# Expert jobs of a hybrid decoder step: the order of the weight splits at a job's start and in the pass of chunk 1

## The chip, the cores and the metric

One core of a Trainium2 chip runs the whole program in one launch. The metric is the device time of one execution in microseconds (us), the median over several runs. The core has a matmul engine (TensorE, "PE" in the profile, its weight loads "PEld"), a vector engine (VectorE, "DVE"), a scalar engine (ScalarE, "ACT"), GpSimd ("POOL") and a sync engine (SyncE, "SP") that here only issues transfers. Each runs its own instructions in program order and waits for the others on semaphores.

## The reference

The kernel computes one step of a two-layer decoder for 256 prompt tokens and 32 sample tokens (288 columns), model width 1024. Layer 0 is a Mamba-2 and sliding-window attention mixer followed by a dense SwiGLU. Layer 1 is an RWKV-7 mixer followed by a mixture of experts, and only this last stage is touched:

```
logits = h @ router                      # 8 experts
top_v, top_i = top_k(logits, 2); gates = softmax(top_v)
for e in range(8):
    y += combine[e] * ((silu(h @ wg[e]) * (h @ wu[e])) @ wd[e])   # 1024 -> 2816 -> 1024, float32
```

## The kernel before

**Jobs and chunks.** The chosen tokens are gathered into jobs of at most 128 rows, each with one expert; with the given inputs there are eight jobs, numbered 0 to 7 here. Job 0 is the first, jobs 1 to 6 are the body of a hardware loop, job 7 is the last and has extra work for the final sum. The expert's hidden width of 2816 is cut into FC = 11 chunks of 256. A chunk's weights are 6144 columns of float32 on 128 partitions: 4096 for gate and up together ("gu", 2 MB) and 2048 for down ("dn", 1 MB). They come into four slots in turn (MS = 4; slot 0 is in the buffer `arena`, the others are in `ring`), by SP's `load_part` (L825 to L831), in the order gu c, dn c-1, gu c+1, and so on. SP waits before each issue until the slot's last user has finished: for gu it is ScalarE that signals this, in its pass of that chunk, after `gu_full`; for dn it is the end of `down`.

**Splits.** TensorE multiplies in a rounded 32-bit format, so every operand is split in two: a head (the rounded value, copied by ScalarE in `heads`, L1411, with its instructions at L1423 for gu and L1418 for dn) and a rest (value minus head, by VectorE in `rests`, L2138, with L2149 for gu and L2143 for dn). Each product is three matmuls: head by head, head by rest, rest by head. A gu chunk is split in two pieces of 2048 columns, numbered 0 and 1; only chunk 0 is split in four pieces of 1024.

**A chunk on TensorE.** `up(c)` is 24 matmuls of 512 columns into bank c mod 2, 12 for each piece. ScalarE takes silu of the gate half (L1486), VectorE multiplies it with the up half (L2291; this also signals `gu_free`). `turn(c)` transposes the product (L3127, two matmuls), ScalarE copies the head of the turned activation (L1493, "turned head" below) and VectorE subtracts for its rest (L2307, "turned rest", signals `tr_free`). `down(c)` is 12 matmuls that add into banks 3 and 4; it waits for the turned rest of its chunk and for the rest of its dn weights. TensorE's order in a job is up(0), up(1), turn(0), up(2), down(0), turn(1), up(3), down(1), turn(2), ... up(10), down(8), turn(9), turn(10), the transposes of the next job's tokens (`turn_tokens`, L3080), down(9), down(10). Then up(0) of the next job follows at once.

**The order on ScalarE and VectorE** is written out by hand in their `job` functions (L1466 and L2282). At the start of a job that is not the first, ScalarE makes the four heads of chunk 0, evicts the finished rows of the previous job (`rows_out`, L1435 and L1436, which waits for the previous job's down(10)), and makes the two heads of chunk 1. VectorE makes the rests of chunk 0 and of piece 0 of chunk 1, then waits for silu(0), multiplies, and makes the rest of piece 1 of chunk 1. After that both go through a loop with one pass for each chunk c: silu or product of chunk c, then head or rest of piece 0 of chunk c+2, the turned activation of chunk c-1, piece 1 of chunk c+2, and a dn part (ScalarE's of chunk c at the end, VectorE's of chunk c-1 near the start). So in the pass of chunk 1 the turned activation of chunk 0 stands behind piece 0 of chunk 3 on both engines, and on VectorE also behind the dn rest of chunk 0.

Of the kernel before, what the change touches and what calls it, by code (L numbers as in the profile page):

```python
# [5 lines left out]
F32 = mybir.dt.float32  # L6
# [3 lines left out]
ALU = mybir.AluOpType  # L10
ACT = mybir.ActivationFunctionType
# [21 lines left out]
FC = FF // 256  # L33
# [96 lines left out]
def decoder_trunk(nc, a, out):  # L130
    with ExitStack() as ctx:
# [5 lines left out]
        def sem(name):  # L137
            if name not in sems:
                sems[name] = ctx.enter_context(nc.semaphore(name))
            return sems[name]  # L140
# [248 lines left out]
        def turned(c):  # L389

            return ps[:, 2 if c % 2 == 0 else 7, 0:256]
# [37 lines left out]
        first = []  # L429
# [607 lines left out]
        def _(act):  # L1037
            A = nc.scalar.activation
# [372 lines left out]
            def heads(j, c, part, pieces):  # L1411

                s = c % MS
                act.wait_ge(sem(f"{part}_loaded{s}"), 16 * (uses[s] * j + c // MS + 1))
                if part == "dn":
                    if c >= 3:
                        act.wait_ge(sem(f"dn_slot_free{(c - 3) % MS}"), uses[(c - 3) % MS] * j + (c - 3) // MS + 2)
                    A(down_head(c), mslot[s][:, GU:SLOT], ACT.Copy).then_inc(sem("dn_head"), 1)  # L1418
                    return
                for i in pieces:  # L1420
                    w = piece_width(c, part)
                    o = i * w
                    A(mhead[c % 2][:, o:o + w], mslot[s][:, o:o + w], ACT.Copy).then_inc(sem("gu_head"), 1)  # L1423
# [7 lines left out]
            def rows_out(j):  # L1431

                act.wait_ge(sem(f"dn_slot_free{(FC - 1) % MS}"), uses[(FC - 1) % MS] * j + 1)
                act.wait_ge(sem("ysb_free"), j)
                A(ysb[:, 0:512], ps[:, 3, :], ACT.Copy)  # L1435
                A(ysb[:, 512:1024], ps[:, 4, :], ACT.Copy).then_inc(sem("y_out"), 1)  # L1436
# [20 lines left out]
            A(gt[:, 1, :], gt[:, 0, :], ACT.Exp).then_inc(sem("gate_exp"), 1)  # L1457
            load_functions(SILU)

            def pair_scale(c):  # L1460

                n = TOK[c][1]
                act.wait_ge(sem(f"pair_loaded{c}"), 32)
                A(pair[0][c][0:n, :], pair[0][c][0:n, :], ACT.Copy, scale=gt[0:n, 2, c:c + 1]).then_inc(sem("pair_scaled"), 1)

            def job(j, first, last=False):  # L1466
                if first:
                    heads(j, 1, "gu", range(2))
                    for u in range(2):
                        token_heads(j, u)  # L1470
                else:
                    heads(j, 0, "gu", range(4))
                    rows_out(j)
                    heads(j, 1, "gu", range(2))
                for c in range(FC + 1):
                    if last and c == 5:
                        act.wait_ge(sem("gather_full"), 2 * j + 3)
                        A(sel_last, ps[:, 5, 0:T], ACT.Copy).then_inc(sem("hsel_head"), 1)
                    if last and c in (4, 6, 9):
                        pair_scale((4, 6, 9).index(c))  # L1480
                    if c < FC:
                        act.wait_ge(sem("gu_full"), FC * j + c + 1)
                        act.sem_inc(sem(f"gu_slot_free{c % MS}"), 1)

                        act.wait_ge(sem("gu_free"), FC * j + c + 2)
                        A(sgm, ps[:, c % 2, 0:256], ACT.Silu).then_inc(sem("silu_ready"), 1)  # L1486
                    if c + 2 < FC:
                        heads(j, c + 2, "gu", range(0, 1))
                    if c == FC - 1:
                        heads(j, c, "dn", range(1))  # L1490
                    if c:
                        act.wait_ge(sem("tr_full"), FC * j + c)
                        A(actTm[(c - 1) % 2][0], turned(c - 1), ACT.Copy).then_inc(sem("tr_head"), 1)  # L1493
                    if c + 2 < FC:
                        heads(j, c + 2, "gu", range(1, 2))
                    if c < FC - 1:
                        heads(j, c, "dn", range(1))
                if last:
                    act.wait_ge(sem("pair_summed"), 2)
                    act.wait_ge(sem("gather_full"), 2 * j + 10)  # L1500
                    A(ysb[:, 0:512], ps[:, 3, :], ACT.Copy).then_inc(sem("y_out"), 1)
                    return
                for u in range(2):
                    token_heads(j + 1, u)
# [10 lines left out]
        def _(dve):  # L1515
            V = nc.vector
# [621 lines left out]
            def rests(j, c, part, pieces):  # L2138

                s, w = c % MS, piece_width(c, part)  # L2140
                if part == "dn":
                    dve.wait_ge(sem("dn_head"), FC * j + c + 1)
                    V.tensor_tensor(mrest[s][:, GU:SLOT], mslot[s][:, GU:SLOT], down_head(c).bitcast(F32),  # L2143
                                    ALU.subtract).then_inc(sem("dn_split"), 1)
                    return
                for i in pieces:
                    o = i * w
                    dve.wait_ge(sem("gu_head"), pieces_to(j, c, part) + i + 1)
                    V.tensor_tensor(mrest[s][:, o:o + w], mslot[s][:, o:o + w], mhead[c % 2][:, o:o + w].bitcast(F32),  # L2149
                                    ALU.subtract).then_inc(sem("gu_split"), 1)  # L2150
# [101 lines left out]
            def last_rows(part):  # L2252
# [10 lines left out]
                                          ALU.is_equal, ALU.mult)  # L2263
                ins.then_inc(sem("pick_ready"), 1)

            def pair_sum(c):

                n = TOK[c][1]
                dve.wait_ge(sem(f"pair_loaded{c}"), 32)
                dve.wait_ge(sem("pair_scaled"), c + 1)  # L2270
                V.scalar_tensor_tensor(pair[0][c][0:n, :], pair[1][c][0:n, :], gt[0:n, 3, c:c + 1], pair[0][c][0:n, :],
                                       ALU.mult, ALU.add).then_inc(sem("pair_summed"), 1)
# [9 lines left out]
            def job(j, first, last=False):  # L2282
                if not first:
                    rests(j, 0, "gu", range(4))
                    rests(j, 1, "gu", range(0, 1))
                for c in range(FC + 1):
                    if c < FC:
                        dve.wait_ge(sem("silu_ready"), FC * j + c + 1)
                        if c >= 2:
                            dve.wait_ge(sem("tr_full"), FC * j + c - 1)  # L2290
                        V.tensor_tensor(actm[c % 2], sgm, ps[:, c % 2, 256:512], ALU.mult).then_inc(sem("gu_free"), 1)  # L2291
                    if last and c in (2, 3):
                        last_rows(c - 2)
                    if last and c in (4, 6, 9):
                        pair_sum((4, 6, 9).index(c))
                    if last and c in (6, 7, 8, 9):
                        pair_add(j, c // 2 - 3, c % 2)
                    if c == 0 and not first:
                        rests(j, 1, "gu", range(1, 2))
                    if 1 <= c <= FC - 2:  # L2300
                        rests(j, c - 1, "dn", range(1))
                    if c + 2 < FC:
                        rests(j, c + 2, "gu", range(0, 1))
                    if c:
                        dve.wait_ge(sem("tr_head"), FC * j + c)
                        hd = actTm[(c - 1) % 2]
                        V.tensor_tensor(hd[1], turned(c - 1), hd[0].bitcast(F32), ALU.subtract).then_inc(sem("tr_free"), 1)  # L2307
                    if c + 2 < FC:
                        rests(j, c + 2, "gu", range(1, 2))
                    if c == FC - 2:  # L2310
                        rests(j, c, "dn", range(1))
                rests(j, FC - 1, "dn", range(1))
                if last:
                    for hf in range(2):
                        pair_add(j, 2, hf)
                    dve.wait_ge(sem("gather_full"), 2 * j + 11)
                    V.tensor_copy(ysb[:, 512:1024], ps[:, 4, :]).then_inc(sem("pair_summed"), 1)
                    for k in range(KT):
                        dve.wait_ge(sem("gather_full"), 2 * j + (12 + k))
                        V.tensor_tensor(x[:, k, :], x[:, k, :], ps[:, DOWN_BANKS[k], 0:T], ALU.add).then_inc(sem("y_final"), 1)  # L2320
                    return
                for u in range(2):
                    token_rests(j + 1, u)
# [959 lines left out]
```

## Time and profile before

| | before |
|---|---|
| median of 3 runs | 1637.08 us (1634.87 to 1638.8) |
| the profiled execution's own time | 1637.31 us |
| its span in the trace | 1634.3 us |
| PE busy | 1590.1 us, 97% |
| DVE busy | 1137.9 us, 70% |
| ACT busy | 896.8 us, 55% |
| chain that ended last | PE 88%, DVE 5%, ACT 2%, DMA 2%, issue 2% |
| mean transfer rate over the span | 248 GB/s |

The span starts with the first instruction and ends with the last; the execution's own time is 3.0 us longer. The expert stage runs from about 816 us to the end, so it is half of the span. "Issue" is idle time whose releaser the profile doesn't show. Busy time of a matmul overlaps with that of the next one, so that starts are the safer numbers: matmuls of 512 columns that don't wait start 0.23 us apart.

### The profile page before, as it was taken

To read this page: it belongs to the slowest core of one execution; us is meant where nothing else is said; L and a number is where in the kernel's file an instruction comes from. 1 tells how busy PE (TensorE), PEld (TensorE's weight loads), DVE (VectorE), ACT (ScalarE), POOL (GpSimd) and SP (SyncE) were. 2 spreads that over 40 slices of the span, in tenths; PEclk is the share of its full clock that TensorE was granted. 3 is DMA by queue.
4 is the path that set the end of the run, shared out by engine and by line. 5 is a ranking of instruction groups with operands and counts; after the bars stand their busy time and mean duration, and the time that the engine had idled before them with its cause. 6 is when DMAs were issued, how large, how long until landed. Compare 5 with 4: busy or idle time off the path is not lost.

```text
span 1634.3 us, 27320 instructions
## 1 busy us (share of the span) xinstructions
PE 1590.1 (97%) x10856; PEld 1309.2 (80%) x10856; DVE 1137.9 (70%) x1476; ACT 896.8 (55%) x1190; POOL 123.3 (8%) x180
## 2 busy tenths in 40 slices
PE   9999999999999999899999999999999999999999
PEld 7766687999998777778767878888787887878787
DVE  4663741677766753335468889797988979798897
ACT  3362541544325353343436777676777767687774
POOL 1104000000000003220222000000000000000100
PEclk9999889999999999998999999999999999999999
DMA  8923533544423240000449999797989979798993
GB/s 334 407 94 124 207 130 123 220 187 170 175 81 119 103 155 1 3 3 2 187 165 395 380 376 412 316 427 305 425 350 376 409 312 426 303 425 347 384 423 121
DMA packets 41103, 404.74 MB, mean 248 GB/s; under 512 B 4784, under 2 KB 5072, under 8 KB 11664
## 3 DMA queue, kind: packets, MB, share of 16 engines
q1 hardware_dynamic: 34336, 372.25, 56.6%
q0 software_dynamic: 6672, 31.14, 4.7%
q8 instruction: 70, 1.15, 0.3%
q14 instruction: 25, 0.20, 0.0%
HBM read 379.09 MB, written 26.30 MB: 248 GB/s over the span
## 4 chain that ended last, share of the span: by engine, by line
PE 88%; DVE 5%; ACT 2%; DMA 2%; issue 2%; POOL 0%; DVEq 0%; ACTq 0%; SPq 0%; POOLq 0%
PE ps L2342 85%; DMA ring<-in_moe_w 1%; PE ps L3127 1%; DMA arena<-in_moe_w 1%; DVE rest_ring L2149 1%; PE ps L2809 1%; PE ps L2750 1%; DVE arena L1688 0%; ACT arena L1270 0%; DVE arena L1701 0%; ACT arena L1283 0%; PE ps L3080 0%; PE ps L2544 0%; DVE h L2057 0%; DVE arena L1776 0%
## 5 line engine op out<-in xcount | busy, mean ns | idle before, releaser
L2342 PE MATMUL ps<-head,hsel 128*128 128x512 f32 x1408 | 457.5, 396 | 2.8 <-DVE rest_ring L2149 2.8
L2342 PEld LDWEIGHTS ps<-head,hsel 128*128 128x128 f32 x1408 | 264.3, 188 | 61.5 <-DVE rest_ring L2149 7.8
L2149 DVE TENSOR_TENSOR rest_ring<-ring,head 128x2048 fp32r<-128x2048 f32 x128 | 291.0, 2284 | 14.4 <-ACT head L1423 14.3
L2342 PE MATMUL ps<-arena,ring 128*128 128x288 f32 (+9 forms) x1408 | 256.6, 347 | 1.3 <-ACT arena L1276 1.2
L1423 ACT ACTIVATE head<-ring 128x2048 fp32r<-128x2048 f32 x128 | 243.1, 1912 | 24.9 <-DMA ring<-in_moe_w 24.9
L2342 PEld LDWEIGHTS ps<-arena,ring 128*128 128x128 f32 (+4 forms) x1408 | 199.5, 189 | 53.1 <-issue 7.7
L2342 PE MATMUL ps<-rest_ring,hsel 128*128 128x512 f32 x512 | 199.6, 390 | 0.0
L2342 PE MATMUL ps<-head,actT_split 128*128 128x512 f32 x512 | 169.1, 394 | 9.0 <-issue 6.3
L2342 PE MATMUL ps<-rest_arena,head 128*128 128x288 f32 x704 | 174.8, 296 | 0.0
L2342 PE MATMUL ps<-rest_arena,rest_ring 128*128 128x288 f32 x528 | 155.5, 294 | 0.0
L2342 PE MATMUL ps<-h,ring 128*128 128x288 f32 (+2 forms) x624 | 133.6, 370 | 3.7 <-ACT h L1332 1.9
L2342 PEld LDWEIGHTS ps<-h,ring 128*128 128x128 f32 (+2 forms) x624 | 99.6, 176 | 37.6 <-issue 10.7
L2342 PEld LDWEIGHTS ps<-head,actT_split 128*128 128x128 f32 x512 | 96.1, 188 | 33.3 <-issue 9.1
L2342 PEld LDWEIGHTS ps<-rest_arena,head 128*128 128x128 f32 x704 | 122.5, 188 | 0.1
L2143 DVE TENSOR_TENSOR rest_ring<-ring,head 128x2048 fp32r<-128x2048 f32 x48 | 109.7, 2285 | 9.7 <-ACT head L1418 9.7
L2149 DVE TENSOR_TENSOR rest_arena<-arena,head 128x1024 fp32r<-128x1024 f32 (+1 forms) x64 | 110.3, 1750 | 3.7 <-ACT head L1423 3.5
L2342 PEld LDWEIGHTS ps<-rest_ring,hsel 128*128 128x128 f32 x512 | 96.4, 188 | 18.0
L2342 PE MATMUL ps<-arena 64*64 64x64 f32 (+13 forms) x1514 | 96.9, 266 | 9.9 <-DVE arena L1721 4.0
L2342 PE MATMUL ps<-hsel,head 128*128 128x288 f32 x352 | 103.8, 295 | 0.0
L1599 DVE TENSOR_TENSOR x<-x,ps 128x288 f32<-128x288 f32 x110 | 48.2, 452 | 77.6 <-PE ps L2342 77.3
L1423 ACT ACTIVATE head<-arena 128x1024 fp32r<-128x1024 f32 (+1 forms) x64 | 92.4, 1485 | 15.9 <-DMA arena<-in_moe_w 15.6
L2342 PE MATMUL ps<-rest_ring,actT_split 128*128 128x512 f32 x256 | 99.7, 389 | 0.0
(387 smaller groups left out, 2283.1 us busy)
## 6 DMA issues: line engine op xcount, KB each, us to landing
ring<-in_moe_w SPq DMA_DIRECT2D x64, 2048.0 KB, 12.4
ring<-in_moe_w SPq DMA_DIRECT2D x64, 1024.0 KB, 8.3
arena<-in_moe_w SPq DMA_DIRECT2D x24, 2048.0 KB, 11.6
arena<-in_moe_w SPq DMA_DIRECT2D x24, 1024.0 KB, 6.6
ring<-in_ffn_w SPq DMA_DIRECT2D x11, 2048.0 KB, 7.4
ring<-in_ffn_w SPq DMA_DIRECT2D x11, 1024.0 KB, 4.8
moe_rows<-arena POOLq DMA_DIRECT2D x1, 6656.0 KB, 34.0
ring<-in_w_in SPq DMA_DIRECT2D x2, 3072.0 KB, 12.8
```

The source lines that it names most:

```text
L1423: A(mhead[c % 2][:, o:o + w], mslot[s][:, o:o + w], ACT.Copy).then_inc(sem("gu_head"), 1)
L1599: V.tensor_tensor(x[:, m, :], x[:, m, :], bank(g)[:, 0:T], ALU.add).then_inc(freesem(g), 1)
L2143: V.tensor_tensor(mrest[s][:, GU:SLOT], mslot[s][:, GU:SLOT], down_head(c).bitcast(F32), ALU.subtract).then_inc(sem("dn_split"), 1)
L2149: V.tensor_tensor(mrest[s][:, o:o + w], mslot[s][:, o:o + w], mhead[c % 2][:, o:o + w].bitcast(F32), ALU.subtract).then_inc(sem("gu_split" ...
L2342: return nc.tensor.matmul(o, l, r, start=start, stop=stop, skip_group_check=skip)
L2750: ins = nc.tensor.transpose(b[0:rows, i * P:(i + 1) * P], src[:, 4 * hf + i, t0:t0 + rows], ident)
L2809: ins = nc.tensor.transpose(b[:, n * P:(n + 1) * P], Mi[gg % 2][:, h0:h0 + 2, :].rearrange("p h t -> p (h t)"), ident)
L3127: ins = nc.tensor.transpose(turned(c)[:, u * P:(u + 1) * P], actm[c % 2][:, u * P:(u + 1) * P], ident)
```

## The change

At the start of a job that is not the first, ScalarE makes the head of piece 0 of chunk 1 ahead of the row eviction, and only piece 1 behind it. VectorE makes both rests of chunk 1 ahead of the product of chunk 0; the rest of piece 1 stood behind it before. In the pass of chunk 1, in all eight jobs, ScalarE makes the turned head of chunk 0 right behind silu(1), ahead of the heads of chunk 3, and VectorE makes the turned rest of chunk 0 right behind the product of chunk 1, ahead of the dn rest of chunk 0 and the rests of chunk 3. The two instructions were put in helper functions with the same content. TensorE's and SP's orders, all shapes and all counts stay.

```
 # ScalarE
+            def turned_head(j, c):
+                act.wait_ge(sem("tr_full"), FC * j + c)
+                A(actTm[(c - 1) % 2][0], turned(c - 1), ACT.Copy).then_inc(sem("tr_head"), 1)
...
                     heads(j, 0, "gu", range(4))
+                    heads(j, 1, "gu", range(0, 1))
                     rows_out(j)
-                    heads(j, 1, "gu", range(2))
+                    heads(j, 1, "gu", range(1, 2))
...
                         A(sgm, ps[:, c % 2, 0:256], ACT.Silu).then_inc(sem("silu_ready"), 1)
+                    if c == 1:
+                        turned_head(j, c)
                     if c + 2 < FC:
                         heads(j, c + 2, "gu", range(0, 1))
                     if c == FC - 1:
                         heads(j, c, "dn", range(1))
-                    if c:
-                        act.wait_ge(sem("tr_full"), FC * j + c)
-                        A(actTm[(c - 1) % 2][0], turned(c - 1), ACT.Copy).then_inc(sem("tr_head"), 1)
+                    if c and not (c == 1):
+                        turned_head(j, c)
 # VectorE
+            def turned_rest(j, c):
+                dve.wait_ge(sem("tr_head"), FC * j + c)
+                hd = actTm[(c - 1) % 2]
+                V.tensor_tensor(hd[1], turned(c - 1), hd[0].bitcast(F32), ALU.subtract).then_inc(sem("tr_free"), 1)
...
                     rests(j, 0, "gu", range(4))
-                    rests(j, 1, "gu", range(0, 1))
+                    rests(j, 1, "gu", range(2))
...
-                    if c == 0 and not first:
-                        rests(j, 1, "gu", range(1, 2))
+                    if c == 1:
+                        turned_rest(j, c)
                     if 1 <= c <= FC - 2:
                         rests(j, c - 1, "dn", range(1))
                     if c + 2 < FC:
                         rests(j, c + 2, "gu", range(0, 1))
-                    if c:
-                        dve.wait_ge(sem("tr_head"), FC * j + c)
-                        hd = actTm[(c - 1) % 2]
-                        V.tensor_tensor(hd[1], turned(c - 1), hd[0].bitcast(F32), ALU.subtract).then_inc(sem("tr_free"), 1)
+                    if c and not (c == 1):
+                        turned_rest(j, c)
```

## Rows read from the trace of the kernel before

**Rows 1.** PE's waits over the expert stage: total us, times, longest.
```profile
PE ps L2342 <- issue: 6.3, 7, 1.6
PE ps L2342 <- DVE rest_ring L2149: 2.8, 7, 0.4
```

**Rows 2.** PE in order of time, job 2: start us, us, instruction, [idle before].
```profile
1059.26 0.50 PE L2342 MATMUL ps<-head,hsel 128*128 128x512 f32 x1 [0.40 <-DVE rest_ring L2149]
...
1062.13 0.38 PE L3127 MATMUL ps<-cst,moe 128*128 128x128 f32 x2
...
1068.78 0.47 PE L2342 MATMUL ps<-head,actT_split 128*128 128x512 f32 x1 [0.80 <-issue]
...
1071.63 0.39 PE L3127 MATMUL ps<-cst,moe 128*128 128x128 f32 x2
```

**Rows 3.** PE's weight loads in order of time, job 2.
```profile
1055.84 0.19 PEld L2342 LDWEIGHTS ps<-head,hsel 128*128 128x128 f32 x1 [0.29 <-DVE rest_ring L2149]
...
1068.75 0.19 PEld L2342 LDWEIGHTS ps<-head,actT_split 128*128 128x128 f32 x1 [1.20 <-issue]
...
1077.08 0.19 PEld L2342 LDWEIGHTS ps<-head,actT_split 128*128 128x128 f32 x1
```

**Rows 4.** ACT in order of time, job 2.
```profile
1045.54 3.90 ACT L1423 ACTIVATE head<-arena 128x1024 fp32r<-128x1024 f32 x4
1050.58 0.60 ACT L1435 ACTIVATE moe<-ps 128x512 f32<-128x512 f32 x1 [1.14 <-PE ps L2342]
...
1051.55 3.72 ACT L1423 ACTIVATE head<-ring 128x2048 fp32r<-128x2048 f32 x2
...
1063.80 1.92 ACT L1423 ACTIVATE head<-ring 128x2048 fp32r<-128x2048 f32 x1 [0.93 <-DMA ring<-in_moe_w]
...
1071.19 1.92 ACT L1423 ACTIVATE head<-arena 128x2048 fp32r<-128x2048 f32 x1 [1.34 <-DMA arena<-in_moe_w]
```

**Rows 5.** DVE in order of time, job 2.
```profile
1048.40 4.62 DVE L2149 TENSOR_TENSOR rest_arena<-arena,head 128x1024 fp32r<-128x1024 f32 x4
1053.50 2.29 DVE L2149 TENSOR_TENSOR rest_ring<-ring,head 128x2048 fp32r<-128x2048 f32 x1 [0.48 <-ACT head L1423]
...
1056.92 6.69 DVE L2149 TENSOR_TENSOR rest_ring<-ring,head 128x2048 fp32r<-128x2048 f32 x3
...
1068.27 0.41 DVE L2307 TENSOR_TENSOR actT_split<-ps,actT_split 128x256 fp32r<-128x256 f32 x1
...
1075.54 0.41 DVE L2307 TENSOR_TENSOR actT_split<-ps,actT_split 128x256 fp32r<-128x256 f32 x1
```

**Rows 6.** Windows: length, busy of PE, PEld, DVE, ACT, POOL, PEclk, DMA share, GB/s.
```profile
1046.00:1114.00 68.00, 66.80 (x300) 54.23 (x299) 62.48 (x44) 53.13 (x44) 0.77 (x2) 1.00 1.01 424
1122.00:1127.00 5.00, 5.00 (x25) 4.10 (x24) 5.00 (x4) 4.00 (x3) 0.00 (x0) 1.00 0.75 259
1527.00:1599.00 72.00, 70.47 (x323) 56.98 (x322) 68.19 (x55) 56.70 (x47) 12.04 (x7) 1.00 1.00 422
```

**Rows 7.** ACT waiting for gu chunks: 4 of jobs 1 and 4, 5 of job 7.
```profile
976.71 1.92 ACT L1423 ACTIVATE head<-arena 128x2048 fp32r<-128x2048 f32 x1 [2.53 <-DMA arena<-in_moe_w]
...
1263.34 1.92 ACT L1423 ACTIVATE head<-arena 128x2048 fp32r<-128x2048 f32 x1 [1.34 <-DMA arena<-in_moe_w]
...
1559.41 1.92 ACT L1423 ACTIVATE head<-ring 128x2048 fp32r<-128x2048 f32 x1 [2.98 <-DMA ring<-in_moe_w]
```

**Rows 8.** PE in order of time: down(1) of job 0, turn(1) of jobs 1 and 4.
```profile
886.11 0.50 PE L2342 MATMUL ps<-head,actT_split 128*128 128x512 f32 x1 [1.10 <-DVE actT_split L2307]
...
976.03 0.38 PE L3127 MATMUL ps<-cst,moe 128*128 128x128 f32 x2
...
1263.46 0.39 PE L3127 MATMUL ps<-cst,moe 128*128 128x128 f32 x2
```

**Rows 9.** SP's issues in order of time, job 2: dn 4, gu 6.
```profile
1071.96 0.33 SPq L830 DMA_DIRECT2D arena<-in_moe_w  x1
1072.47 0.33 SPq L830 DMA_DIRECT2D ring<-in_moe_w  x1
```

## The prediction

> **What bounds the kernel now.** I read the page's shares first: PE is busy for 97% of the span and makes up 88% of the chain that ended last, so an edit pays only where PE stands still. Next I read PE's waits over the expert stage [rows 1]. There are seven waits of 2.8 us in total for the rest of a gu piece, and seven called "issue" of 6.3 us in total: one of each for every job that isn't the first. Job 2 in order of time shows where they are [rows 2], and the weight loads show two of them more sharply, because a load stands just ahead of its matmul [rows 3]. Three places are late in each such job:
> - A: the first load of up(1) comes at 1055.84 after 0.29 us idle, where loads that don't wait have some 0.04 between them, so it is 0.25 late.
> - B: up(1) stops at its middle, 1059.26, for the rest of piece 1.
> - C: down(0) starts at 1068.78 after 0.80 us idle, "issue".
>
> Then ACT and DVE over the same stretch [rows 4, 5] tell why. A and B: ACT has made the heads of chunk 0 by 1049.44 (1045.54 + 3.90), then waits 1.14 for the previous job's down(10) before the row eviction, and begins chunk 1 only at 1051.55. DVE idles 0.48 for that head, ends the rest of piece 0 at 1055.79, and piece 1 only at about 1059.2, since the product stands between them. C: the profile names nobody, but DVE's turned rest ends at 1068.68 (1068.27 + 0.41) and down(0)'s load follows 0.07 later. That rest stands behind the rest of piece 0 of chunk 3, which stands behind its head on ACT, which waited for a transfer until 1063.80.
>
> **The cost of each stall, with its restart.** Matmuls of 512 columns start 0.227 us apart. From a turn to the load of the down behind the next up it takes 1077.08 - 1071.63 = 5.45 us when nothing waits [rows 2, 3].
> - A and B: without A the first load of up(1) is at 1055.60, its matmul at 1055.82, and 24 x 0.227 = 5.44 later turn(0) starts, at 1061.26. It starts at 1062.13: 0.87 us.
> - C: turn(1) starts 9.50 after turn(0) [rows 2]; without a wait it is 5.45 + 0.22 from load to matmul + 12 x 0.227 = 8.40 to 8.43. So 1.07 us.
>
> Together 1.94 us a job. The period of a loop job is 1071.63 - 976.03 = 95.60 [rows 2, 8].
>
> **The change, part by part, in the times of job 2.** (1) ACT's head of piece 0 of chunk 1 starts at about 1049.35 and ends at 1051.25; this fills a gap in which ACT waited. The eviction (two copies, 0.97 us from 1050.58 to 1051.55) moves from 1050.58 to 1051.15. Behind it stand the head of piece 1, now 1052.12 to 1054.03, and GpSimd's store of the rows. The head has an end 1.2 us earlier than before (1055.27), and down(0), which waits for the eviction, comes 14 us later, so I cost the delay at nothing. If that cover went it would be 0.57 us. (2) DVE goes on without its 0.48 gap: chunk 0's rests end at 1053.02, piece 0 is done at 1055.22 (2.29 us, with 0.08 overlap), 0.3 ahead of the load at 1055.60, and piece 1 at 1057.42, ahead of its load at 1058.3. A and B go. (3) The price is that the product of chunk 0 waits for piece 1: 1057.34 in place of 1056.59. Behind its `gu_free` stand up(2), turn(0) and silu(1), the first of them at 1061.26, so 3.5 us of cover. The rests of chunk 2 end at 1062.90, 0.7 us earlier than before (1063.61), because their heads are ready at 1058.36. (4) In the pass of chunk 1, ACT's silu(1) starts at 1061.87, behind the dn head. turn(0), at 1061.26, can be read from about 1061.7. The turned head takes 1062.15 to 1062.51 and adds no wait, because ACT idled until 1063.80 there. (5) DVE's product(1) ends at 1063.24, the turned rest at 1063.57, the dn rest at 1065.78. down(0)'s load is due at 1061.26 + 5.45 = 1066.71: both are ahead by 0.9 us, so C goes. The rests of chunk 3 end at 1070.25, where up(3) wants the first at 1069.9 and has it at 1068.05.
>
> The bounds: where the trace doesn't show the new order, A, B and C can each cost between nothing and what they cost now (0.13, 0.74 and 1.07 by the working above). I take nothing for each, since the margins (0.3, 0.9, 0.9 us) are positive.
>
> **What is late next.** down(1). Its turned rest still stands behind the rest of piece 0 of chunk 4, and that behind the arrival of chunk 4 at 1071.19 [rows 4]. From arrival to the load of down(1) it takes 1.95 for the head, 2.21 for the rest, 0.42 for the turned rest and 0.07, together 4.65 us: 1075.84. Before, the load was due at 1077.08 and had 1.2 us to spare. Now it is due 1.94 earlier, at 1075.14, so it is 0.70 late, of which PE loses about 0.62 (C: load 1.15 late, PE 1.07). The arrival doesn't come earlier with PE: from 1046 to 1114 the transfer engines are busy all the time, share 1.01 at 424 GB/s [rows 6], and the stream starts with slots that down(8) and down(9) of the previous job free, ahead of anything saved. A chunk of 3.146 MB takes 7.4 us at this rate (1063.80 to 1071.19) against 8.43 on PE, so each later chunk has 1 us more to spare, and the next (down(2)) already has 0.9. At the job's end the engines are at 0.75 [rows 6], so PE sets the pace again and the next job starts its stream as much earlier as PE is.
>
> One rule of the Trainium skill would speak against all of this. "DMA: Bandwidth & Descriptors", Where 436 GB/s comes from, says that for loads from HBM the side of some 358 GB/s per core binds. By that figure the 34.6 MB of a job would take an estimated 96.6 us, over the period of 95.60, and no order of the splits would gain anything. The trace doesn't agree for this one core alone: it holds 424 GB/s for 68 us. So the sum goes by the measured rate, at which the job's weights take 34.6/0.424 = 81.6 us.
>
> **The sum.** Jobs 2, 3, 5 and 6 repeat the pattern, with arrivals of chunk 4 within 0.3 us of each other relative to turn(1); they gain 1.32, 1.56, 1.41 and 1.36. Job 1: chunk 4 arrives at 976.71, 1.2 us later relative to turn(1) (976.03) than in job 2 [rows 7, 8]. Ready at 981.36, due at 976.03 + 5.45 - 1.88 = 979.60, lost 1.68, gain 0.20. Job 4: C was larger (1.86), arrival 1263.34, ready 1267.99, due at 1263.46 + 5.45 - 2.73 = 1266.18, lost 1.73, gain 1.0. Job 0: only the pass of chunk 1 changes; down(0) gains 1.4, and down(1) waits for the same arrival as before (it idled 1.10 at 886.11 [rows 8]), so 0. Job 7: 1.94 is saved early, but its transfer engines are at 1.00 for 72 us [rows 6], as the row gathers come on top, chunk 5 arrives only at 1559.41 [rows 7], and down(2) waits for it already; so 0. Sum: 0.20 + 1.32 + 1.56 + 1.0 + 1.41 + 1.36 = 6.85 us. The profiled execution's own time of 1637.31 becomes 1630.5; it lies 0.2 above the median of the runs, which becomes 1630.2. I say 1630.3. With 0.5 us of play for each of the six gains it is 1627.3 to 1633.3.
>
> **Rivals.** About 0.2% (3.3 us) is what a measurement of this kernel can tell from no change.
> - *All given back at down(1).* The arrival of chunk 4 decides, and in each job it comes as late as in job 1: 0.2 a job, 7 x 0.2 = 1.4, 1635.7. For it: job 1, and the spread of C. Against: four of six loop jobs lie within 0.3 us of each other. Chance 0.16.
> - *The arrivals move with PE*, so that nothing is given back: 7 x 0.87 + 1.01 + 1.86 + 5 x 1.07 = 14.3, 1622.8. Against: the saturated windows. Chance 0.06.
> - *Slower: the earlier issue slows the transfer ahead of it.* down(0) ends 1.9 us earlier, so SP issues dn 4 and gu 6 earlier [rows 9], while gu 5 is on its way. If the engines shared their rate between them, gu 5 would come later. down(2) has 0.9 us to spare, and from there each us costs one. Half a chunk's time, 3.7 us, costs 2.8 in each of six jobs, 16.8, less the 6.9: 1647. Against: before, too, these issues lie at 1071.96 and 1072.47 with gu 5 landing at 1078.6, a plain 7.4 after gu 4. Chance 0.06.
> - *It doesn't do what it says*: one of the margins of 0.3 to 0.9 is used up by waits that I can't see, and A, B or C stays in part; with C whole and A, B gone it is 6 x 0.87 less nothing given back, 5.2, 1632, inside my range and part of the forecast's 0.72.
>
> **How the numbers follow.** Forecast 0.72, arrivals with PE 0.06, given back 0.16, slower 0.06. Nearly all of the first lies over the 3.3 us (say 0.70 of 0.72), with the second that is 0.76 faster; 0.17 same; 0.07 slower. The range goes from 1625.5, toward the second rival, to 1635.5, nearly all of the first; it holds 8 in 10.
>
> **What the changed profile would show.** In jobs 1 to 7 no idle time of PE at the middle of up(1) or before down(0); turn(0) 0.87 earlier in the job. A new wait before down(1), for DVE's turned rest (L2307), of some 0.3 to 0.4 us idle in four jobs and over 1 in jobs 1 and 4. A period of 94.3. ACT still waits for the arrivals of chunks 3, 4 and 5, which come at the same distance from the previous job's end. In job 0 no wait before down(0) and a wait of some 2.5 us before down(1). I am wrong if chunk 4 arrives at another distance, or if PE stops elsewhere, at down(2) or in up(3).

## The result and the profile after

| | before | after |
|---|---|---|
| median of 20 runs each | 1636.51 us | 1626.79 us |
| ratio, 95% interval | | 0.9944 [0.9924, 0.9965] |
| the profiled execution's own time, its span | 1637.31, 1634.3 us | 1622.35, 1620.0 us |
| granted clock over the span | 0.987 | 0.992 |

The change makes the kernel faster by 0.56%: by the ratio that is 9.2 us, with an interval from 5.7 to 12.4. The forecast was a gain of 6.85 us, which lies in that interval, and a time of 1630.3 in a range of 1625.5 to 1635.5, in which 1626.79 lies, near its lower end.

The two profiled executions lie 14.3 us apart in span, more than the change is worth. To see what belongs to it, I cut the expert stage at marks that both kernels have: the transposes of the next job's tokens (L3080 before, L3091 after), once in each job. These are the marks of the trace after, PE in order of time; the columns are as in rows 2.

```profile
941.94 1.04 PE L3091 MATMUL ps<-cst,moe 128*128 128x128 f32 x8
...
1037.18 1.04 PE L3091 MATMUL ps<-cst,moe 128*128 128x128 f32 x8
...
1132.42 1.04 PE L3091 MATMUL ps<-cst,moe 128*128 128x128 f32 x8
...
1226.57 1.04 PE L3091 MATMUL ps<-cst,moe 128*128 128x128 f32 x8
...
1320.36 1.04 PE L3091 MATMUL ps<-cst,moe 128*128 128x128 f32 x8
...
1414.37 1.04 PE L3091 MATMUL ps<-cst,moe 128*128 128x128 f32 x8
...
1508.15 1.04 PE L3091 MATMUL ps<-cst,moe 128*128 128x128 f32 x8
```

And the first and the last of before:

```profile
948.35 1.04 PE L3080 MATMUL ps<-cst,moe 128*128 128x128 f32 x8
...
1522.28 1.04 PE L3080 MATMUL ps<-cst,moe 128*128 128x128 f32 x8
```

The loop of six jobs takes 1508.15 - 941.94 = 566.21 us, against 573.93: 7.72 us less. Its periods are 95.24, 95.24, 94.15, 93.79, 94.01 and 93.78, against 95.58, 95.45, 95.61, 96.23, 95.61 and 95.45. From the last mark to the end it is 111.9 against 112.0, and from turn(0) of job 0 to the first mark 79.00 against 79.03. So the stage gains 7.9 us. The other 6.4 us between the spans lie ahead of turn(0) of job 0, in code that the change doesn't touch. There the granted clock differs, 0.99 after and 0.98 before; from turn(0) of job 0 on it is 1.00 in both.

From 845 us on, all of PE's waits after the change are of one kind (total us, times, longest). The two lines of rows 1 no longer occur:

```profile
PE ps L2353 <- DVE actT_split L2277: 7.0, 7, 2.5
```

The kernel before had waits of this kind too, which rows 1 leave out: two in job 0 and one in job 7.

```profile
PE ps L2342 <- DVE actT_split L2307: 2.6, 3, 1.1
```

Job 3, which is one with an early arrival, in order of time: PE, ACT, DVE. Rows 2, 4 and 5 show the same places before.

```profile
1149.75 0.38 PE L3138 MATMUL ps<-cst,moe 128*128 128x128 f32 x2
...
1158.18 0.38 PE L3138 MATMUL ps<-cst,moe 128*128 128x128 f32 x2
...
1164.24 0.50 PE L2353 MATMUL ps<-head,actT_split 128*128 128x512 f32 x1 [0.19 <-DVE actT_split L2277]
```

```profile
1139.63 0.58 ACT L1435 ACTIVATE moe<-ps 128x512 f32<-128x512 f32 x1
1140.10 0.60 ACT L1436 ACTIVATE moe<-ps 128x512 f32<-128x512 f32 x1
...
1150.61 0.38 ACT L1463 ACTIVATE actT_split<-ps 128x256 fp32r<-128x256 f32 x1
1152.20 3.72 ACT L1423 ACTIVATE head<-ring 128x2048 fp32r<-128x2048 f32 x2 [1.21 <-DMA ring<-in_moe_w]
...
1159.60 1.92 ACT L1423 ACTIVATE head<-arena 128x2048 fp32r<-128x2048 f32 x1 [1.61 <-DMA arena<-in_moe_w]
```

```profile
1145.83 0.41 DVE L2304 TENSOR_TENSOR moe<-moe,ps 128x256 f32<-128x256 f32 x1
...
1151.62 0.42 DVE L2277 TENSOR_TENSOR actT_split<-ps,actT_split 128x256 fp32r<-128x256 f32 x1
1151.95 2.28 DVE L2150 TENSOR_TENSOR rest_arena<-arena,head 128x2048 fp32r<-128x2048 f32 x1
...
1161.56 2.29 DVE L2156 TENSOR_TENSOR rest_arena<-arena,head 128x2048 fp32r<-128x2048 f32 x1 [0.38 <-ACT head L1423]
1163.77 0.42 DVE L2277 TENSOR_TENSOR actT_split<-ps,actT_split 128x256 fp32r<-128x256 f32 x1
```

turn(0) comes 17.33 us after the mark (18.20 before, in job 2 of rows 2), and turn(1) 8.43 after turn(0) (9.50): A, B and C are gone. As forecast, the row eviction starts 0.56 us later in the job and the product of chunk 0 starts 0.75 later, and nothing waits for either. The turned rest of chunk 0 ends at 1152.04, with the arrival of chunk 3 at 1152.20 no longer ahead of it. What is late next is the turned rest of chunk 1, at 1164.19: it follows the rest of chunk 4, which follows its head, which waited for chunk 4 until 1159.60. In jobs 4 to 6 the idle time at this place is too short for the view, but turn(2) still comes 8.68 to 8.77 after turn(1), where it takes 8.40 to 8.43 without a wait. The transfer engines are still saturated here (length, busy of PE, PEld, DVE, ACT, POOL, granted clock, DMA share, GB/s):

```profile
1134.00:1200.00 66.00, 65.81 (x296) 53.82 (x295) 61.91 (x44) 52.59 (x45) 1.07 (x2) 1.00 1.01 425
```

### The profile page after: what moved, and what is told of

Its sections match the earlier page's. It is cut to its first block, busy times and chain, and to the rows that moved or that the text cites. A ratio compares the mean times of both kernels' runs of the same rounds, so it can differ in the third digit from the quotient of the medians.

```text
span 1620.0 us, 27320 instructions
## 1 busy us (share of the span) xinstructions
PE 1578.7 (97%) x10856; PEld 1304.4 (81%) x10856; DVE 1137.9 (70%) x1476; ACT 893.9 (55%) x1190; POOL 122.6 (8%) x180
## 3 DMA queue, kind: packets, MB, share of 16 engines
q8 instruction: 70, 1.15, 0.3%
## 4 chain that ended last, share of the span: by engine, by line
PE 85%; DMA 6%; DVE 4%; ACT 3%; issue 2%; POOL 0%; DVEq 0%; SPq 0%; ACTq 0%; POOLq 0%
PE ps L2353 81%; DMA arena<-in_moe_w 5%; DMA ring<-in_moe_w 1%; PE ps L3138 1%; PE ps L2820 1%; ACT head L1423 1%; PE ps L2761 1%; DVE arena L1695 0%; ACT arena L1270 0%; DVE arena L1708 0%; ACT arena L1283 0%; PE ps L3091 0%; PE ps L2555 0%; DVE arena L1783 0%; DVE h L2064 0%
## 5 line engine op out<-in xcount | busy, mean ns | idle before, releaser
L2156 DVE TENSOR_TENSOR rest_ring<-ring,head 128x2048 fp32r<-128x2048 f32 x128 | 290.4, 2284 | 18.2 <-ACT head L1423 17.7
L2353 PE MATMUL ps<-arena,ring 128*128 128x288 f32 (+9 forms) x1408 | 253.3, 344 | 1.2 <-ACT arena L1276 1.2
L2353 PEld LDWEIGHTS ps<-head,actT_split 128*128 128x128 f32 x512 | 96.1, 188 | 30.8 <-DVE actT_split L2277 10.6
L2353 PEld LDWEIGHTS ps<-rest_ring,hsel 128*128 128x128 f32 x512 | 96.4, 188 | 18.4
## 6 DMA issues: line engine op xcount, KB each, us to landing
ring<-in_moe_w SPq DMA_DIRECT2D x64, 2048.0 KB, 13.7
```

The source lines that it names most:

```text
L2353: return nc.tensor.matmul(o, l, r, start=start, stop=stop, skip_group_check=skip)
```

## The experiments

Each was profiled once; the ones with a ratio were timed too. The loop of six jobs is taken between the same marks, where the granted clock is 1.00 in all of them but rest_moved_alone, and this is the number that compares them to some tenths of a us.

| kernel | mark to turn(0) | turn(0) to turn(1), early / late job | loop of six |
|---|---|---|---|
| before | 18.2 | 9.5 / 9.4, 10.3 | 573.93 |
| after | 17.3 | 8.4 / 8.4 | 566.21 |
| after, once more | 17.3 | 8.4 / 8.4 | 566.16 |
| start_only | 17.3 | 9.7 to 9.9 / 10.7, 10.9 | 571.87 |
| turned_only | 18.2 | 8.4 / 8.4 | 568.38 |
| turned_12 | 17.3 | 8.4 / 8.4 | 562.60 |
| late_rows | 17.3 | 8.4 / 8.4 | 561.89 |
| before_late_rows | 18.2 | 9.5 / 9.5 | 573.29 |
| rest_moved_alone | 17.3 | 10.1 to 10.3 / 12.4, 11.2 | 580.56 |
| all_ahead | 17.3 | 8.4 / 8.4 | 561.59 |

A chunk's arrival is read from the moment when ScalarE, waiting for it, begins its head. A "late" job is one where chunk 4 arrives 28.0 to 28.5 us after the mark, against 26.9 to 27.3 in the others. Each trace in which these arrivals show has two of them among the six loop jobs: before jobs 1 and 4, after 1 and 2, all others 1 and 3. Chunk 3 is late in them too, but for job 1 of before and of turned_only, where ScalarE begins chunk 3 at 19.8 as in an early job. That is why the kernel before has 9.4 in one late job and 10.3 in the other.

**start_only**: one half of the change.

```
-                    if c == 1:
+                    if c == -1:
                         turned_head(j, c)      # ScalarE; the same for turned_rest on VectorE
...
-                    if c and not (c == 1):
+                    if c:
                         turned_head(j, c)      # behind piece 0 of chunk c+2, as before
```

> Only the new order at a job's start (head of piece 0 of chunk 1 ahead of the row eviction, both rests of chunk 1 ahead of the product of chunk 0); the turned activation of chunk 0 stands behind chunk 3 as before. My theory (the turned rest of chunk 0 is held by the arrival of chunk 3, so what the start saves is mostly given back at down(0)): from the next-token transposes to turn(0) 17.3 us in place of 18.2, from turn(0) to turn(1) about 10.0 in place of 9.5, period about 95.3 in place of 95.6, loop of six jobs 2 us shorter. Rival (the stalls are independent and add): turn(0) to turn(1) stays 9.5, period 94.7, loop 5.2 us shorter.

Measured: 17.34 to turn(0), C grown to 9.74 to 9.93 between the turns (10.65 and 10.85 in the late jobs), loop 2.06 us shorter. The stalls are not independent: of the 0.87 that the start saves, the arrival of chunk 3 takes back 0.2 to 0.4 at down(0). In the late jobs 1 and 3 (periods 95.89 and 96.10) it takes back 0.4 and 0.6 against job 4 of before, whose chunk 3 was late too (10.27, period 96.23). In all six loop jobs turn(1) comes 7.49 to 7.52 us after ScalarE begins chunk 3, and in job 4 of before 7.53; in the other jobs of before it comes 7.8 to 8.1 after it, so there something else held it (before_late_rows shows what). PE's waits from 845 us on; "issue" is C:

```profile
PE ps L2353 <- issue: 9.7, 7, 2.1
PE ps L2353 <- DVE actT_split L2277: 3.3, 4, 1.2
```

**turned_only**: the other half.

```
                 if not first:
                     rests(j, 0, "gu", range(4))
-                    rests(j, 1, "gu", range(2))
+                    rests(j, 1, "gu", range(0, 1))
...
+                    if c == 0 and not first:
+                        rests(j, 1, "gu", range(1, 2))      # and rows_out ahead of both heads on ScalarE
```

> Only the turned activation of chunk 0 moved ahead; the start of a job as before. My theory: 18.2 us to turn(0) as before, 8.43 from turn(0) to turn(1), down(1) without a wait where chunk 4 arrives at 27.2 us after the next-token transposes (period 94.5), and with a wait of about 0.9 for its load where it arrives at 28.4 (period 95.4). Loop of six jobs 5 to 6.5 us shorter than before. Rival (the two parts need each other): under 2 us.

Measured: 18.2 to turn(0), 8.42 from turn(0) to turn(1), periods of 94.4 to 94.5 and in the late jobs 95.39 and 95.28 with a wait of 0.4 to 0.5 before down(1); loop 5.55 us shorter. So the turned activation's place is the larger half. The two halves add up to 7.6 of 7.7, but that doesn't make the stalls independent. The start gives 2.1 alone and 2.2 on top of turned_only, in place of six times 0.87, since an arrival takes the rest back, at down(0) in the one and at down(1) in the other.

**turned_12**: the changed kernel with one pass more.

```
-                    if c == 1:
+                    if c in (1, 2):
                         turned_head(j, c)      # and turned_rest; "c not in (1, 2)" in the other place
```

> The changed kernel with the turned activation moved ahead in the pass of chunk 2 as well (chunk 1's turned head and rest ahead of chunk 4's split). My theory (down(1) waits only because its turned rest stands behind the split of chunk 4, which waits for its arrival): no wait before down(1) in any job, period 93.5 where chunk 4 arrives at 27.0 and 94.2 where it arrives at 28.3 (then down(2) waits 0.6 for chunk 5), loop of six 561 to 563.5 us against 566.2; job 0 0.6 to 0.9 us shorter. Rival (ScalarE now waits for turn(1) ahead of the heads of chunk 4, and these come late): no gain or slower, with a wait of PE in up(4).

Measured: no wait of PE before down(1) in any job. Periods are 93.50, 93.50, 93.67 and 93.51 in the early jobs; 94.46 and 93.96 in the late ones, where down(2) is late in turn (0.49 us idle in job 1). Loop 562.60, 3.6 under the changed kernel. The feared price, that chunk 4's heads come late because ScalarE waits for turn(1) ahead of them, is nowhere in the trace: the heads begin when the chunk lands, and PE waits in no up. Job 0 could not be compared, for a reason given in the last section. What follows: the wait before down(1) is one of place in the queue behind an arrival.

**late_rows**: the arrival itself moved.

```
             with pool.Fori(1, jl) as j:
+                pool.wait_ge(sem("gu_full"), FC * j + 7)
                 next_rows(j)
                 store_rows(j)
```

> The changed kernel with GpSimd's two row transfers of a loop job (512 KB in, 512 KB out) held until chunk 6's up is done, out of the stretch at a job's start in which the transfer engines are saturated. My theory (arrival of chunk 4 is set by the bytes queued since the previous job's down(8)): chunks 3 and 4 arrive up to 2.4 us earlier, 24.6 to 26 us after the next-token transposes in place of 27.0 to 28.4, no wait before down(1) in jobs 1 to 6, period 93.5, loop of six about 561 us against 566.2. Rival (the weights' own queue sets the arrival): chunk 4 arrives at 27.0 as before and nothing changes.

Measured: chunk 4 arrives 24.5 us after the mark in the early jobs and 25.7 to 25.8 in the late ones, the view shows no wait of PE in the six loop jobs, the periods are 93.58 to 93.72, the loop is 561.89. GpSimd's two transfers are issued 58 us after the mark; in the changed kernel they were issued 2 and 9 us after it. This is ACT in job 4, whose mark is at 1231.63; the chunk came 24.56 us after it, in the trace of after at 26.94:

```profile
1255.50 0.39 ACT L1493 ACTIVATE moe<-ps 128x256 f32<-128x256 f32 x1
1256.19 1.92 ACT L1424 ACTIVATE head<-arena 128x2048 fp32r<-128x2048 f32 x1 [0.30 <-DMA arena<-in_moe_w]
```

1 MB of row traffic moved out of the stretch brings the weights 2.4 us forward, and 1.05 MB at 424 GB/s take 2.5. So the arrival is set by the bytes queued since down(8) of the previous job.

**before_late_rows**: the same edit to the kernel before.

> The kernel before with GpSimd's two row transfers of a loop job held until chunk 6's up is done, so that chunks 3 and 4 arrive 2.4 us earlier (as late_rows showed). My theory (in the kernel before C is held by the order of VectorE's queue, product(1), dn rest 0, rest of chunk 3, turned rest, all back to back, and only in the late jobs by the arrival): turn(0) to turn(1) stays at 9.5 in every job, also in those that showed 10.3, period 95.5, loop of six 573.1 against 573.9. Rival (C is a wait for the arrival of chunk 3, through the engines): turn(0) to turn(1) falls to 8.4 to 8.7, loop 5 to 6 us shorter.

Measured: 9.49 to 9.52 between the turns in all jobs, loop 573.29. With the arrivals 2.4 us earlier, the kernel before gains 0.6 us only, in what was its late job 4. So in the kernel before, C in most jobs was VectorE's own queue, and the arrival stood close behind it; only after the start is quicker (start_only) does the arrival decide in every job. My prediction had put C on the arrival of chunk 3 in its first part.

**rest_moved_alone**: the changed kernel with ScalarE's half of the second part undone.

```
-                    if c == 1:
+                    if c == -1:
                         turned_head(j, c)      # ScalarE only
...
-                    if c and not (c == 1):
+                    if c:
                         turned_head(j, c)
```

> The changed kernel with VectorE's turned rest moved ahead and ScalarE's turned head left behind piece 0 of chunk 3. My theory (both engines' orders have to change together): VectorE waits at the head of its queue for a turned head that waits for chunk 3's arrival; the dn rest of chunk 0 ends at about 24.8 us after the next-token transposes in place of 21.9, down(0) waits about 1.9 us, down(1) a further 1.2; turn(0) to turn(1) 10.3, turn(1) to turn(2) 9.5, period over 96.5, slower than before. Rival (VectorE's order alone matters): as the changed kernel, period 93.8 to 95.2.

Measured: loop 580.56, 6.6 us slower than before. DVE in job 4, mark at 1244.07: it stands 2.63 us at the turned rest, with the dn rest of chunk 0 behind it, for which down(0) now waits.

```profile
1262.97 0.41 DVE L2304 TENSOR_TENSOR moe<-moe,ps 128x256 f32<-128x256 f32 x1
1266.01 0.43 DVE L2277 TENSOR_TENSOR actT_split<-ps,actT_split 128x256 fp32r<-128x256 f32 x1 [2.63 <-ACT actT_split L1463]
1266.35 2.28 DVE L2150 TENSOR_TENSOR rest_arena<-arena,head 128x2048 fp32r<-128x2048 f32 x1
```

```profile
PE ps L2353 <- DVE rest_arena L2150: 10.9, 6, 2.5
PE ps L2353 <- DVE actT_split L2277: 6.0, 8, 1.5
```

The waits came where they were expected, a little smaller in the early jobs: PE idles 1.4 to 1.6 before down(0) and 0.7 before down(1), turn(0) to turn(1) takes 10.1 to 10.3, the period is 96.2 to 96.4 in place of over 96.5. Of the 12.42 us in job 1 some 1.3 are the clock: down(0) starts there 25.71 us after the mark, in job 3 at 25.68, but in job 1 its matmuls run in part at 1.2 GHz (granted clock 0.50) after PE had idled 2.53 us, and turn(1) comes 1.27 later than in job 3, where PE had idled 2.46 and the clock stayed at 2.4 GHz (1.00). So the orders alone cost some 5.3 of the 6.6 us. The window over that stretch, columns as in rows 6:

```profile
980.00:982.00 2.00, 2.00 (x6) 1.48 (x5) 2.00 (x2) 1.42 (x1) 0.00 (x0) 0.50 1.09 463
```

VectorE's order changed without ScalarE's loses more than the whole change gains. The other half, ScalarE's order alone, was not run; before_late_rows, in which C stayed with VectorE's queue while the arrivals came earlier, lets one expect that it would leave C. A slower outcome was close by, and none of my rivals had it.

**all_ahead**: late_rows, and the turned activation ahead wherever a chunk is late.

```
+                ahead = range(1, 8) if first else range(1, 6) if last else range(1, 3)
...
-                    if c == 1:
+                    if c in ahead:
                         turned_head(j, c)      # and turned_rest
```

> The changed kernel with the row transfers held as in late_rows and the turned activation ahead of the coming chunk in the passes of chunks 1 to 7 of job 0, 1 and 2 of a loop job, 1 to 5 of the last job. My theory (every wait that is left in the expert stage is a turned rest behind the split of a chunk that hasn't arrived): from turn(0) of job 0 to the next-token transposes 76.2 us in place of 79.0 where TensorE's clock was full before it (76.2 as before where it wasn't), loop of six 561.9 against 566.2, from the last next-token transposes to the end 109.9 against 111.9, the whole 6 to 9 us under the changed kernel, near 1619. Rival (the engines wait for turn(c) with the chunk's split behind it, and an up comes late): no gain over late_rows in job 0 and job 7, with waits of PE in an up.

Measured: 0.9892 of before, interval [0.9855, 0.9930], median 1621.22 of 9 runs; the medians of this and the next lie 8.5 us apart, as expected. Its loop, 561.59, is the shortest of these kernels. The traces show 5 us of the 8.5 against after_again (4.6 in the loop, 0.4 in the last job); the rest is not accounted for. The last job missed: from its mark to the end 111.2 where I expected 109.9. The waits before down(1) to down(3) went, but two others took their place, one at down(5) and one in front of the transposes of the row pairs for the final sum:

```profile
PE ps L2356 <- DVE actT_split L2279: 0.9, 1, 0.9
PE ps L3115 <- ACT moe L1486: 0.3, 1, 0.3
```

So my theory, that each wait left is a turned rest behind a chunk's split, held in the loop and not in the last job. Job 0 took 76.2 from turn(0) to the mark, but at a lower clock ahead of it, so what the new order does there at full clock was not seen. What it gains over late_rows in the whole time was not measured: late_rows was profiled once, and the loops differ by 0.3 us only.

**after_again**:

> The changed kernel once more, on the chip of all_ahead and beside the same runs of the kernel before. By 20 runs each it was 0.9944 of before; by the trace of the expert stage (7.9 us) it is 0.9952. I expect 0.993 to 0.997, and a loop of six between 562 and 568 us by how many jobs have a late arrival of chunk 4.

Measured: 0.9947 [0.9926, 0.9969], median 1629.71 of 12 runs beside 1636.99 of before; loop 566.16. Both are as expected.

## Why the prediction was right, step by step

- *A and B go, 0.87 a job*: 18.20 became 17.33 in all seven jobs. Right. Row eviction and product of chunk 0 moved back at no cost. The prediction's bounds give A 0.13 and B 0.74; its working yields only their sum, and no run takes them apart.
- *C goes, 1.07*: 8.43 between the turns. Right in size. That the profile's "issue" hides a turned rest held by an order on DVE was right too. That the arrival of chunk 3 was its cause was wrong in most jobs: before_late_rows left C whole. The sum didn't rest on it, since it took C from PE's starts.
- *Given back at down(1)*: right in place, cause and about in size. The six jobs gained 0.34, 0.21, 1.46, 2.44, 1.60 and 1.67 against 0.20, 1.32, 1.56, 1.0, 1.41 and 1.36 forecast. Jobs 2 and 4 are off because the late arrivals fell on jobs 1 and 2 in place of 1 and 4; this cancels. That it cancels is luck: why two jobs in six are late, and which, is open, and in the changed kernel a late job takes 1.1 to 1.5 us longer (95.24 against 93.78 to 94.15). What is left, 7.72 against 6.85, is nearly all in the early jobs, if each is compared with an early one: chunk 4 came at 26.93 to 27.18 after the mark in place of 27.03 to 27.27, over the four of them 0.6 us in all, and each tenth of that counts for PE. So the prediction's sign of being wrong, chunk 4 at another distance, came true by 0.1 to 0.3 us in the early jobs and by over 1 us in jobs 2 and 4, without harm to the sum. turned_12 and late_rows show the cause in two independent ways.
- *Job 0 nothing*: its stalls of 1.15 and 1.10 became one of 2.53 before down(1), and 79.03 became 79.00. Right. *Job 7 nothing*: 0.1. Right; chunks 5 and 6 came 36.7 and 46.6 us after the mark (37.1 and 46.8 before), and waits before down(1), down(2) and down(3) took back all but that.
- *The rivals.* "All given back" is refuted by four of six jobs and true of the two late ones, which gained 0.34 and 0.21. "Arrivals move with PE" would have brought chunk 4 some 1.9 us earlier, to about 25.3 us after the mark in an early job; it came at 26.9 and later. Refuted. "The earlier issue slows the transfer ahead of it": SP's issues of dn 4 and gu 6 came 26.1 and 26.6 us after the mark in place of 28.0 and 28.5, and chunk 5 still came 7.4 after chunk 4 in all loop jobs. Refuted. "It doesn't do what it says": PE waits at none of the three places, so the margins held. But its price for C whole with A and B gone, 5.2 us with nothing given back, was wrong: start_only is that kernel and gains 2.06 in the loop.
- *The median.* The stage gains 7.9 in the trace; the ratio gives 9.2 with 3.4 either way. The difference isn't resolved. The time came out 3.5 us under the 1630.3: 0.6 of it because the median of the kernel before was 1636.51 in place of 1637.08, 1.0 because the stage gained 7.9 in place of 6.85, and the rest open.

## What to carry to other kernels

When a stall is removed from a chain that another resource feeds at its own rate, compute the slack at the next consumer of that resource first: here 1.94 us were saved a job and the next consumer had 1.2 in hand. An instruction that holds up the bottleneck should not stand in a queue behind one that waits for a transfer; but move it on all engines of its chain, or the one that is moved can wait at the head of its queue and block what is behind it, as in rest_moved_alone. When profiles of two kernels are compared, cut them at marks inside the stage that was changed.

## What the runs showed of the hardware

**The clock at the start of the expert stage.** The first 48 matmuls of job 0's gather took 8.48 us in four of the ten traces and 13.5 to 13.7 in the other six, the changed kernel being in both groups. These are the changed kernel's in its two profiles, each followed by the window over that stretch (the last number but two is the granted clock):

```profile
843.50 8.48 PE L2353 MATMUL ps<-arena 128*128 128x128 f32 x48 [1.23 <-ACT arena L1454]
```

```profile
843.50:857.00 13.50, 13.50 (x70) 10.71 (x71) 9.03 (x30) 5.94 (x5) 0.00 (x0) 1.00 0.89 355
```

```profile
852.39 13.64 PE L2353 MATMUL ps<-arena 128*128 128x128 f32 x48 [1.23 <-ACT arena L1454]
```

```profile
852.39:866.00 13.61, 13.61 (x49) 10.33 (x49) 5.09 (x3) 5.45 (x4) 0.00 (x0) 0.56 0.88 347
```

The clock is at 2.4 GHz in the first (1.00) and for most of the stretch at 1.2 GHz in the second (0.56), after the same small pieces of work with a gap of 1.2 us. From the first of these matmuls to the end the two profiles of the same kernel take 776.5 and 781.1 us: the lower clock costs 7.6 us up to turn(0) (27.07 from the first of them in place of 19.44), of which 2.8 come back by the first mark, since job 0 then finds its chunks arrived and doesn't wait (76.2 from turn(0) to the mark, against 79.0). This spread of 4.6 us is over half of what the change is worth. Why it falls in one execution and not in another is open.

**Two late jobs.** Chunk 4, and mostly chunk 3 too, comes some 1.2 us late in two loop jobs of a trace, with the same issue times on SP, to 0.1 us. It does so in late_rows too (25.7 against 24.5), where GpSimd's rows are out of the stretch, so these aren't the cause. In job 2 of after the transfer that SP issues 0.4 us after the mark already lands late, at 12.06 in place of 10.6 to 10.9; in job 1 of after that one is in time (10.66), and a later one is late. What the cause is stays open; no experiment was made on it.
